# Attention scores in two steps instead of four, and the first turn of probabilities one k-step later, in a two-layer streaming encoder

## The reference, cut to what matters

```
logits = einsum('bqhmd,bkhmd->bhmqk', qi, k) * scale
logits = where(mask, logits + bias[:, None], NEG)
p = softmax(logits, axis=-1)
p = p[:, :, 0] - lam_full * p[:, :, 1]
o = einsum('bhqk,bkhd->bqhd', p, v)
```

## Time and profile before

| | us |
|---|---|
| median of 3 runs (lowest, highest) | 1279.24 (1277.55, 1280.09) |
| profiled execution | 1279.51 |
| its span, first to last instruction | 1277.7 |
| TensorE busy | 1248.9 |
| VectorE busy | 705.6 |
| ScalarE busy | 562.3 |
| GpSimd busy | 530.8 |

### The profile page before, as it was taken

One profiled execution on the slowest core, in us unless ns is written; L12 is line 12 of the kernel. 1 busy time (PEld: TensorE's weight loads), 2 busy tenths in 40 slices (PEclk: granted clock), 3 DMA queues, 4 the chain that ended last, 5 costly groups with the idle time before them and its releaser, 6 DMA issues.

```text
span 1277.7 us, 17071 instructions
## 1 busy us (share of the span) xinstructions
PE 1248.9 (98%) x5560; PEld 990.0 (77%) x5560; DVE 705.6 (55%) x1163; ACT 562.3 (44%) x899; POOL 530.8 (42%) x265
## 2 busy tenths in 40 slices
PE   8999999989999999999999999999999999999996
PEld 7777777667888888888888777668788888888884
DVE  5557776763776733346887799972533333331002
ACT  4356656643533344442224555663544444442221
POOL 2143332122334444444452577734244444444440
PEclk7899999999999999999998999999999999999998
DMA  8553444222355522236673221202122222232321
GB/s 335 194 180 116 148 148 164 100 99 66 132 197 189 172 85 97 93 106 230 235 244 102 76 67 67 66 17 94 71 98 91 92 97 95 89 106 96 105 85 66
DMA packets 44919, 156.78 MB, mean 123 GB/s; under 512 B 4936, under 2 KB 5192, under 8 KB 44880
## 3 DMA queue, kind: packets, MB, share of 16 engines
q1 hardware_dynamic: 44816, 156.27, 35.4%
q10 hardware_dynamic: 64, 0.02, 0.0%
HBM read 154.15 MB, written 2.12 MB: 122 GB/s over the span
## 4 chain that ended last, share of the span: by engine, by line
PE 88%; DVE 5%; issue 2%; ACT 2%; DMA 2%; SPq 0%; DVEq 0%; ACTq 0%
PE psum L909 26%; PE psum L910 25%; PE psum L911 25%; PE psum L1251 3%; PE psum L920 1%; DVE psum L1486 1%; DVE pt_lo L1495 1%; PE psum L939 1%; DMA bias<-rel_scratch 1%; PE psum L976 1%; PE psum L1080 1%; DVE acc L1337 1%; DMA ada_first<-ada_w 1%; PE psum L1107 1%; PE psum L1119 0%
## 5 line engine op out<-in xcount | busy, mean ns | idle before, releaser
L496 POOL TENSOR_TENSOR w_lo<-w_raw,w_hi 128x1024 fp32r<-128x1024 f32 (+1 forms) x192 | 455.9, 2391 | 703.2 <-ACT w_hi L580 702.9
L909 PE MATMUL psum<-h_hi,w_hi 128*128 128x512 f32 x1152 | 467.9, 406 | 4.2 <-DVE x L1590 2.2
L910 PE MATMUL psum<-h_lo,w_hi 128*128 128x512 f32 x1152 | 451.8, 392 | 0.0
L911 PE MATMUL psum<-h_hi,w_lo 128*128 128x512 f32 x1152 | 451.8, 392 | 0.0
L909 PEld LDWEIGHTS psum<-h_hi,w_hi 128*128 128x128 f32 x1152 | 218.6, 190 | 55.8 <-issue 8.5
L910 PEld LDWEIGHTS psum<-h_lo,w_hi 128*128 128x128 f32 x1152 | 218.4, 190 | 47.0 <-issue 4.9
L911 PEld LDWEIGHTS psum<-h_hi,w_lo 128*128 128x128 f32 x1152 | 218.1, 189 | 46.8
L580 ACT ACTIVATE w_hi<-w_raw 128x1024 fp32r<-128x1024 f32 (+1 forms) x192 | 195.6, 1032 | 73.6 <-DMA w_raw<-w_tiles 73.3
L909 PE MATMUL psum<-a_hi,w_hi 128*128 128x512 f32 x352 | 137.1, 390 | 0.8 <-issue 0.8
L911 PE MATMUL psum<-a_hi,w_lo 128*128 128x512 f32 x352 | 137.0, 389 | 0.0
L910 PE MATMUL psum<-a_lo,w_hi 128*128 128x512 f32 x352 | 136.9, 389 | 0.0
(11 more groups left out here) (190 smaller groups left out, 1364.1 us busy)
## 6 DMA issues: line engine op xcount, KB each, us to landing
w_raw<-w_tiles SPq DMA_DIRECT2D x160, 512.0 KB, 3.3
ada_buf<-ada_w SPq DMA_DIRECT2D x32, 512.0 KB, 3.3
w_raw<-w_tiles SPq DMA_DIRECT2D x32, 448.0 KB, 3.1
ada_late<-ada_w SPq DMA_DIRECT2D x28, 512.0 KB, 5.2
ada_mid<-ada_w SPq DMA_DIRECT2D x20, 512.0 KB, 4.5
ada_first<-ada_w SPq DMA_DIRECT2D x16, 512.0 KB, 9.5
x<-x_in SPq DMA_DIRECT2D x4, 512.0 KB, 6.7
bias<-rel_scratch SPq DMA_DIRECT2D x1, 2048.0 KB, 10.8
```

The source lines that it names most:

```text
L496: nc.gpsimd.tensor_tensor(w_lo[:, slot, 0:k], w_raw[:, (ph.tile + l) % 2, 0:k], f(w_hi[:, slot, 0:k]), ALU.subtract).then_inc(lo_done, 1)
L909: nc.tensor.matmul(dst, w_hi[:, slot, k], rhs_hi, start=first, stop=False)
L910: nc.tensor.matmul(dst, w_hi[:, slot, k], rhs_lo, start=False, stop=False)
L911: return nc.tensor.matmul(dst, w_lo[:, slot, k], rhs_hi, start=False, stop=last)
```

## The change

Behind step 0 TensorE now has the scores of tiles 0 and 1, tile 1 in columns 128 to 383 of the same two banks. Behind step 2 it has those of tiles 2 and 3: tile 2 in bank 2 (free between the copy of v and the next product for v) and bank 6, tile 3 in banks 3 and 4. `turn_v` stands alone behind step 1, and `turn_p(0)` moves from behind step 3 to behind step 4. Logits 0 wait for the scores of tile 1 too. Some waits are added, others fall away. In the last head the projection's chunk that stood behind gap 3 stands behind gap 4; the order of its turns and chunks is otherwise kept.

```
+        def score_at(i, mp):
+            w = P * (i + 1)
+            if i == 2:
+                return psum[:, 2 if mp == 0 else PT + 1, 0:w]
+            return psum[:, SC + mp, P:P + w] if i == 1 else psum[:, SC + mp, 0:w]
...
                 pe.wait_ge(v_copied, h)
+                pe.wait_ge(sc_read, lin(it, SC0 + 8 * c + 5, 16))
...
                     for mp in range(2):
-                        pe.wait_ge(sc_read, lin(it, SC0 + 8 * c + 2 * i + mp - 1, 16))
+                        if i == 0:
+                            pe.wait_ge(sc_read, lin(it, SC0 + 8 * c + mp - 1, 16))
+                        if i == 2 and mp:
+                            entry_free(1)
+                        if i == 3:
+                            pe.wait_ge(sc_read, lin(it, SC0 + 8 * c + 3 + mp, 16))
...
-                        dst = psum[:, SC + mp, 0:w]
+                        dst = score_at(i, mp)
...
                     entry_free(1 + i)
+                    if i == 0:
+                        pe.wait_ge(sc_read, lin(it, SC0 + 8 * c + 6, 16))
...
-                return {0: (lambda: scores(0),), 1: (turn_v, lambda: scores(1)), 2: (lambda: scores(2),),
-                        3: (lambda: scores(3), lambda: turn_p(0)), 5: (lambda: turn_p(1),), 7: (lambda: turn_p(2),),
+                return {0: (lambda: scores(0), lambda: scores(1)), 1: (turn_v,),
+                        2: (lambda: scores(2), lambda: scores(3)), 4: (lambda: turn_p(0),), 5: (lambda: turn_p(1),), 7: (lambda: turn_p(2),),
                         10: (lambda: turn_p(3),), 12: (output,), 14: (ada,), 15: (mean_square,)}
...
-            chunks = {0: ((0, 0),), 1: ((0, 1),), 2: ((0, 2),), 3: ((0, 3),), 5: ((0, 4),), 7: ((0, 5), (0, 6)),
+            chunks = {0: ((0, 0),), 1: ((0, 1),), 2: ((0, 2),), 4: ((0, 3),), 5: ((0, 4),), 7: ((0, 5), (0, 6)),
...
-                dve.wait_ge(sc_done, lin(it, 8 * c + 2 * i + 2, 16))
+                dve.wait_ge(sc_done, lin(it, 8 * c + (4 if i == 0 else 2 * i + 2), 16))
...
-                    V.tensor_tensor_reduce(z_of(i, mp), psum[:, SC + mp, 0:w],
+                    V.tensor_tensor_reduce(z_of(i, mp), score_at(i, mp),
```

## The result

| | before | after |
|---|---|---|
| median of 6 runs (lowest, highest) | 1276.89 (1275.17, 1280.09) | 1284.16 (1283.19, 1287.27) |
| profiled execution | 1279.51 | 1283.28 |
| its span | 1277.7 | 1281.5 |
| TensorE busy | 1248.9 | 1242.7 |

The account below looks back on a forecast made before the run. A chain without slack in each head, from turn 0 through ScalarE's copy and 7.64 us of VectorE work to turn 3, bounds the kernel. 1279.51 + 4.9 - 0.5 = 1283.9 profiled, stated as 1283.6 us, range 1281.5 to 1289.5.

Parts of the forecast that it names:

- TensorE's own stream: In each head, merged steps and transposes left alone shorten TensorE's work by 0.55 to 0.77 us.
- Turn 0 later: In each head, turn 0 queued one k-step later starts 0.64 to 0.86 us later, taken as 0.70.
- VectorE's idle time: Ahead of tile 0's remainder, VectorE's wait grows from 0.73 to about 1.4 us a head, over 10 in all.
- Turn 2 waits: In each head, TensorE waits about 0.4 us at turn 2 and about 1.1 us at turn 3.
- Turn 0 to turn 3 stays 8.45: In each head, turn 3 still follows turn 0 by 8.45 us, through ScalarE's copy and VectorE's work.
- Seven heads: Heads 0 to 6 each become 0.70 us longer, +4.9 us in all, bounds 4.5 and 6.0.
- The last head: The last head gains 0 to 1.05 us from an earlier turn 0, taken as 0.5.
- Logits 0 later: In each head, logits 0 come about 0.5 us later by waiting for step 1, hidden behind ScalarE's L754.
- A: Rival: turn 3 isn't held by the chain from turn 0, TensorE's shorter stream counts; 1273.8 us, chance 0.09.
- B: Rival: joints between merged steps save nothing, turn 0 comes 1.35 us later; +9.0, 1288.2 us, chance 0.10.
- D: Rival: delay and saving cancel, no difference; 1278.7 to 1281 us, chance 0.05.
- C: Rival: TensorE's waits make its clock fall, 1.7 us each; 1287 to 1289, or 1295.5 in all seven heads; chance 0.15.

Follow-up runs that it names:

- e1: Changed kernel with turn 0 put back behind step 3, scores still merged; 1274.65 us against 1278.85 for the kernel before, ratio 0.9965.
- e2: Kernel before with only turn 0 moved behind step 4, no step merged; 1287.85 us against 1278.85 for the kernel before, ratio 1.008.
- e7: Kernel before with only the scores of tiles 0 and 1 merged and turn_v alone behind step 1; 1276.92 us against 1278.94, ratio 0.9988.
- e3: Changed kernel with VectorE's ada(0) put ahead of the remainder of tile 0; 1280.88 us against 1278.85 for the kernel before, ratio 1.0017.
- e4: Kernel before with VectorE's ada(0) put ahead of the remainder of tile 0; 1277.34 us against 1278.85 for the kernel before, ratio 0.9995.
- e9: e1 with VectorE's logits 1, mix 0 and ada 0 drawn forward; 1273.33 us against 1278.82 for the kernel before, ratio 0.9963.
- e10: Changed kernel run once more for a second profile, nothing edited; 1283.93 us against 1277.05 for the kernel before, ratio 1.0054.
- e6: e1 with VectorE's ada(1) moved behind the remainder of tile 3; 1320.16 us against 1278.94 for the kernel before, ratio 1.0321.
- e5: e1 with ada(1) behind the remainder of tile 3 and TensorE's ada product behind mean_square; 1302.53 us against 1278.94 for the kernel before, ratio 1.0177.

## Why the prediction was right

The heads shown, side by side (us, worked out from the starts in the timelines; the third number is the head less the first two):

| kernel | to turn 0 | turn 0 to turn 3 | turn 3 to the head's end | head |
|---|---|---|---|---|
| before | 8.18 | 8.45 | 9.18 | 25.81 |
| changed | 8.94 | 8.39 | 9.19 | 26.52 |
| e1 | 7.57 | 8.39 | 9.21 | 25.17 |
| e2 | 9.71 | 8.40 | 9.19 | 27.30 |
| e7 | 7.91 | 8.45 | 9.20 | 25.56 |
| e3 | 8.95 | 7.93 | 9.18 | 26.06 |
| e4 | 8.19 | 8.32 | 9.04 | 25.55 |
| e9 | 7.55 | 8.27 | 9.03 | 24.85 |

The first five rows have VectorE's order as it was, and their last two parts agree within 0.1 us: the head is the time of turn 0 plus 17.6. When turn 0 comes decides, and the rest of the change acts only through it. The last three rows change VectorE's order and shorten the second part; where the waits at turn 3 have gone (e4, e9) the output's wait shrinks as well, and the third part with it.

- *TensorE's own stream shorter by 0.55 to 0.77 us, 0.49 to 0.71 of it by turn 0:* confirmed. By turn 0, e1 (same step as before) is 8.18 - 7.57 = 0.61 us ahead, of which e7 shows 0.27 for tiles 0 and 1 with `turn_v`. The rest, 0.34, is the merge of tiles 2 and 3 with turn 0 alone.
- *Turn 0 later by 0.64 to 0.86, taken 0.70:* 0.76 in the trace. A k-step between cost 8.94 - 7.57 = 1.37 in the changed kernel (1.35 forecast), and 9.71 - 8.18 = 1.53 in e2, where the scores of tile 3 and turn 0 became two separate steps.
- *VectorE's idle time 0.73 to about 1.4:* 1.42; over 10 us in all: 13.1.
- *Turn 2 waits about 0.4, turn 3 about 1.1:* 0.43 and 1.02.
- *Turn 0 to turn 3 stays 8.45:* 8.39, since ScalarE's copy now follows turn 0 by 0.31 us instead of 0.37. So of 0.76 the head got about 0.70. That the value taken for turn 0's delay, 0.70, is also the head's is partly luck: two misses of 0.06 cancel.
- *Seven heads, +4.9 us:* 4.8 in the first profile.
- *The last head, -0.5:* wrong in size and, in the first profile, in sign. The part I left open in that step ("the L1334 ahead of it may then be held as well") is what happened: the wait moved from the second ada part to the first, and 0.29 us of the 0.8 came through to VectorE's pair. The step that failed is the next one, taking VectorE's gain straight to the head's end: from turn 2 to turn 3 TensorE's own products at the lower clock come last, and they took back 0.3 us in e10 and 1.0 in the first profile. The Trainium skill's "SBUF — State Buffer", section "SBUF: two separate sides", names operations with two SBUF inputs or in a two-port mode; L1350 has one tensor input and took 2.20 us beside GpSimd, so by the rule it runs in such a mode, and the trace agrees with the lock but doesn't show the mode.
- *Logits 0 later, hidden:* e1 and e7 have the same later logits 0, and their heads are shorter by all that turn 0 came earlier. Nothing of it showed.

Sum for the profiled execution: 1279.51 + 4.8 + 0.7 - 1.7 = 1283.3 against 1283.28 measured and 1283.9 forecast. Two terms outside the heads cancelled in part: the last head (+0.7 instead of -0.5) and the clock at 700 us (-1.7, not forecast). That is luck, and so is part of the agreement of the time itself. 1283.6 stood on a median of 1279.24, a rise of 4.4 us, and 1284.16 is 7.3 above the median of the same comparison. By the ratio the rise is 3.7 to 7.7 us, which takes in the 4.8 of the heads; in the second comparison it is 4.7 to 9.1. There the clock of each run is on record too. Span times mean granted clock, which takes half of the low-clock time off, averages 1256.1 us in the nine runs of the changed kernel and 1251.7 in the twelve of the kernel before: 4.4 apart. The other 2.2 us between the mean times (6.6) go with the clock, 0.979 against 0.981. Whether the change has a part in that difference of the clock these runs don't show.

The rivals: A (faster, the chain doesn't hold turn 3) falls with e2, in which the delay of turn 0 alone costs 1.49 us in each head, and with the constant 8.4 us. B (the joints save nothing) falls with the joint at 125.90 and with e1. D needs slack behind L1495; none showed in e2 either, where turn 0 comes 1.53 us later and the head is 1.49 longer. C didn't happen in the changed kernel, where the granted clock stays at 1.00 in heads 0 to 6, with TensorE busy for 25.23 of 26.52 us; e6 shows that its mechanism exists with longer waits. The swing of the clock under frequent short idles, of which the Trainium skill speaks in "TensorE: Matmul & The Clock Gate", section "A second HAM failure mode: psum-queue depth-cycling", has no instance here at waits of 0.4 and 1.0 us. The Trainium skill's advice on eight banks ("Perfetto Trace Analysis", section "Matmul Optimizations") doesn't separate the two kernels, though the prediction set it beside rival A: the kernel before also uses all eight, and the change only gives banks 2 and 6 a second use. e1 places its scores in the same banks as the changed kernel and is 0.35% faster, the changed kernel 0.44% slower.

## What to carry to other kernels

Before a saving on the busiest engine is counted, look for stretches of another engine that run without a gap into a wait of the first; there the time of the instruction that starts the stretch decides, and everything saved around it only makes the wait longer. When steps are merged, keep such an instruction at its old place or earlier (e1). Work that is ready can fill the idle time ahead of the stretch (e3 and e4: heads shorter by 0.46 and 0.26 us), until another engine's queue holds the stretch, as ScalarE's does in e3. Work that can be moved later by its data may still hold a buffer for which a transfer waits (e5, e6).

## What the runs showed of the hardware

- Pairs of matmuls on 64 rows each run on from one query tile's scores into the next with no gap (0.19 and 0.23 us between starts), also into another bank.
- VectorE's L1350, one tensor from SBUF and a scalar per partition, takes 0.48 us alone. Beside GpSimd's subtraction in the last head it took 2.20, 2.19 in e10 and 2.62 in e9, and ended about 0.3 us behind GpSimd each time.
- The clock fell to its lower level 2.6 to 3.8 us into the same 48 one-column matmuls in all eleven profiles (in the kernel before at 693.47, in the changed one at 700.07), though the profile counts TensorE as busy without a break there. It stayed low for 6.83 us in the two profiles in which the fall came latest (3.7 and 3.8 us in) and for 10.24 in the other nine. No run leaves these matmuls out, so that they are the cause is not shown. The length makes 1.7 us between two executions, a third of the effect of this change, so a difference of this size is to be read from stretches and not from one span.
